# A fourth seven-product block in the second and third column group of w_in

## The reference, cut to what matters

```python
h = rms_norm(x, attn_norm)
z = h @ w_in
r_q, r_k, r_v, r_g, c_q, c_kv, k_pe, g_u, g_v = jnp.split(z, IN_SPLITS, axis=-1)
```

## Time and profile before

| | us |
|---|---|
| median of 3 runs | 1095.73 (1095.42 to 1097.48) |
| profiled execution | 1095.72 |
| its span, first to last instruction | 1093.4 |
| TensorE busy | 1078.3 |
| VectorE busy | 911.8 |
| ScalarE busy | 652.9 |
| GpSimd busy | 55.7 |

### The profile page before, as it was taken

The page is one execution under the profiler, slowest core; times in us unless marked ns, Lnnn a source line. Parts: engine busy times, 40 slices in busy tenths (PEclk is TensorE's granted clock), DMA queues, the critical chain, the costliest instruction groups (busy, mean ns, idle before and its releaser), DMA issues.

```text
span 1093.4 us, 12415 instructions
## 1 busy us (share of the span) xinstructions
PE 1078.3 (99%) x5094; PEld 896.6 (82%) x5094; DVE 911.8 (83%) x859; ACT 652.9 (60%) x638; POOL 55.7 (5%) x54
## 2 busy tenths in 40 slices
PE   9999999999999999999999999999999999999997
PEld 6888889987888877788888888888888778888886
DVE  6879666754566798999999999999999799999994
ACT  7666547665655566655656656556665655565652
POOL 0078000000000000000000000000000000000000
PEclk9999999999999999999999999999999999999999
DMA  8765544644355577677677677677674755555552
GB/s 327 281 236 195 193 135 131 203 156 139 130 180 170 190 269 225 236 231 236 218 237 223 208 241 221 224 234 221 234 234 159 303 192 197 195 205 205 199 195 112
DMA packets 50295, 227.50 MB, mean 208 GB/s; under 512 B 4288, under 2 KB 10176, under 8 KB 28736
## 3 DMA queue, kind: packets, MB, share of 16 engines
q1 hardware_dynamic: 47936, 213.84, 57.2%
q0 software_dynamic: 1440, 10.49, 4.8%
q10 hardware_dynamic: 864, 2.39, 0.6%
HBM read 222.51 MB, written 4.19 MB: 207 GB/s over the span
## 4 chain that ended last, share of the span: by engine, by line
PE 88%; DVE 6%; ACT 2%; DMA 2%; issue 1%; SPq 0%; DVEq 0%; ACTq 0%
PE ps L1676 67%; PE ps L1529 5%; PE ps L1531 5%; PE ps L1530 5%; PE ps L1568 2%; DMA raw<-in_w_dn 1%; DVE w_lo L1239 1%; DVE t_lo L1268 1%; ACT t_hi L747 1%; PE ps L1616 1%; DVE t_sum L1253 1%; PE ps L1793 1%; PE ps L1795 1%; PE ps L1794 1%; PE ps L1615 0%
## 5 line engine op out<-in xcount | busy, mean ns | idle before, releaser
L1676 PE MATMUL ps<-w_hi,xp_hi 128*128 128x512 f32 x404 | 159.8, 395 | 1.8 <-DVE ps L1371 0.7
L966 DVE TENSOR_TENSOR w_lo<-raw,w_hi 128x2048 fp32r<-128x2048 f32 (+2 forms) x42 | 87.3, 2078 | 86.4 <-ACT w_hi L490 86.4
L1676 PE MATMUL ps<-w_hi,xp_lo 128*128 128x512 f32 x404 | 157.5, 390 | 0.0
L1676 PE MATMUL ps<-w_lo,xp_hi 128*128 128x512 f32 x404 | 157.4, 390 | 0.0
L747 ACT ACTIVATE t_hi<-t_sum 128x2048 fp32r<-128x2048 f32 x44 | 84.4, 1918 | 73.3 <-DVE t_sum L1258 73.3
L830 ACT ACTIVATE w_hi<-raw 128x2048 fp32r<-128x2048 f32 (+1 forms) x44 | 79.1, 1798 | 79.7 <-DMA raw<-in_w_dn 79.7
L1676 PE MATMUL ps<-w_hi,xo_hi 128*128 128x512 f32 x292 | 113.9, 390 | 2.1 <-DVE xo_lo L1431 2.1
L1676 PE MATMUL ps<-w_lo,xo_hi 128*128 128x512 f32 x292 | 113.6, 389 | 0.0
L1676 PE MATMUL ps<-w_hi,xo_lo 128*128 128x512 f32 x292 | 113.6, 389 | 0.0
L1268 DVE TENSOR_TENSOR t_lo<-t_sum,t_hi 128x2048 fp32r<-128x2048 f32 x44 | 100.7, 2289 | 6.6 <-ACT t_hi L747 6.6
L490 ACT ACTIVATE w_hi<-raw 128x2048 fp32r<-128x2048 f32 (+2 forms) x42 | 73.0, 1738 | 50.4 <-DMA raw<-in_w_out 25.6
(11 more groups left out here) (294 smaller groups left out, 2456.9 us busy)
## 6 DMA issues: line engine op xcount, KB each, us to landing
raw<-in_w_gu SPq DMA_DIRECT2D x78, 1024.0 KB, 5.0
raw<-in_w_dn SPq DMA_DIRECT2D x44, 1024.0 KB, 4.9
raw<-in_w_i SPq DMA_DIRECT2D x21, 1024.0 KB, 4.9
raw<-in_w_out SPq DMA_DIRECT2D x16, 1024.0 KB, 5.1
raw<-in_w_in SPq DMA_DIRECT2D x12, 1024.0 KB, 5.1
d_raw<-in_w_gu SPq DMA_DIRECT2D x10, 1024.0 KB, 4.8
d_lo<-in_w_gu POOLq DMA_DIRECT2D x10, 1024.0 KB, 11.7
raw<-in_w_in SPq DMA_DIRECT2D x8, 576.0 KB, 3.8
```

What stands on the lines that cost most here:

```text
L966: nc.vector.tensor_tensor(w_lo[n % 4][:, 0:k, 0:c], raw[n % 4][:, 0:k, 0:c], w_hi[n % 4][:, 0:k, 0:c].bitcast(F32), ALU.subtract).then_inc ...
L1676: mm = nc.tensor.matmul(out, x, wt, start=start and j + m == 0, stop=stop and 3 * j + m == n - 1, skip_group_check=resumed)
```

## The change

The pair that stood last in groups 1 and 2 (pair 4) moves to position 5 and becomes a fourth seven-product block, so that positions 0, 2, 4 and 5 are such blocks. Its activation sums are a fourth `xi`, made in group 0. The mixing moves from steps 4 and 5 to step 5, and the operations of `in_lo(n + 3)` are spread between the parts of the mixing. TensorE now waits for the mixed banks at position 7, the last chunk of the group. VectorE gets one more wait: the sums of position 5 use the buffers of position 2, so they wait until TensorE has used that chunk.

```diff
-IN_ORDER = [list(range(8))] + [[5, 0, 6, 1, 7, 2, 3, 4]] * 2
-IN_SUMS = (5, 6, 7)
+IN_ORDER = [list(range(8))] + [[5, 0, 6, 1, 7, 4, 2, 3]] * 2
+IN_SUMS = (5, 6, 7, 4)
+IN_AT = (0, 2, 4, 5)
...
-    return (g - 1) * NI + p // 2 if g and p < 5 and p % 2 == 0 else None
+    return (g - 1) * NI + IN_AT.index(p) if g and p in IN_AT else None
...
                 if n == FB - AHEAD:
                     x_sums_hi(2)
-                if g and p == 4:
+                    x_sums_hi(3)
+                if g and p == IN_AT[-1]:
                     act.wait_ge(in_mix_done, 2 * (g - 1) + 1)
...
-            def in_lo(n):
+            def in_lo(n, parts="swl"):
...
+                if "s" in parts:
+                    dve.wait_ge(raw_in[slot], 16 * (n // 4 + 1))
+                    if n % FB == IN_AT[-1]:
+                        dve.wait_ge(chunk_used, n - IN_AT[-1] + IN_AT[1] + 1)
...
+            x_sums(3)
             x_sums_lo(2)
+            x_sums_lo(3)
             for n in range(FB - AHEAD, C0):
                 g, p = divmod(n, FB)
-                if g and p == 4:
+                if g and p == IN_AT[-1]:
                     in_mix_sums(g)
+                    if n + AHEAD < C0:
+                        in_lo(n + AHEAD, "s")
                     in_mix_banks(g, 0)
-                if g and p == 5:
+                    if n + AHEAD < C0:
+                        in_lo(n + AHEAD, "w")
+                    else:
+                        low(n + AHEAD, c=width(n + AHEAD))
                     in_mix_banks(g, 1)
-                if n + AHEAD < C0:
+                    if n + AHEAD < C0:
+                        in_lo(n + AHEAD, "l")
+                elif n + AHEAD < C0:
                     in_lo(n + AHEAD)
...
-                    if g and p == 6 and b == 0:
+                    if g and p == IN_AT[-1] + 2 and b == 0:
                         pe_.wait_ge(in_mixed, 2 * (g - 1) + half + 1)
```

More of the change, by code:

```diff
@@ L163, in build @@
         xi = [at(f"xi{i}", 64 * K + 4 * K * i, [8, P]) for i in range(NI)]
-        xi_hi = [at(f"xi_hi{i}", H0 + 51 * K + 512 + 4 * K * i, [4, P], F32R) for i in range(NI)]
-        xi_lo = [at(f"xi_lo{i}", H0 + 53 * K + 512 + 4 * K * i, [4, P], F32R) for i in range(NI)]
+        XI_AT = [H0 + 51 * K + 512 + 4 * K * i for i in range(3)] + [152 * K]
+        xi_hi = [at(f"xi_hi{i}", XI_AT[i], [4, P], F32R) for i in range(NI)]
+        xi_lo = [at(f"xi_lo{i}", XI_AT[i] + 2 * K, [4, P], F32R) for i in range(NI)]
         mix_in = at("mix_in", 144 * K, [4, COLS])
@@ L1052, in in_lo @@
                 b12, b22, b21 = raw[slot][:, 0, :], raw[slot][:, 2, :], raw[slot][:, 3, :]
[L1053 to L1065, removed]
+                if "s" in parts:
+                    dve.wait_ge(raw_in[slot], 16 * (n // 4 + 1))
+                    if n % FB == IN_AT[-1]:
+                        dve.wait_ge(chunk_used, n - IN_AT[-1] + IN_AT[1] + 1)
+                    nc.vector.tensor_tensor(t_in[:, 0:2, :], raw[slot][:, 1:3, :],
+                                            b12.unsqueeze(1).to_broadcast([P, 2, COLS]), ALU.add).then_inc(in_sum_step, 1)
+                    dve.wait_ge(in_sum_step, 3 * s + 1)
+                    nc.vector.tensor_tensor(t2, t1, b22, ALU.add).then_inc(in_sum_step, 1)
+                    dve.wait_ge(in_sum_step, 3 * s + 2)
+                    nc.vector.tensor_tensor(t4, t2, b21, ALU.add).then_inc(in_sum_step, 1)
+                if "w" in parts:
+                    dve.wait_ge(in_sum_step, 3 * s + 3)
+                    dve.wait_ge(hi_ready, n + 1)
+                    nc.vector.tensor_tensor(w_lo[slot][:, 1:4, :], raw[slot][:, 1:4, :], w_hi[slot][:, 1:4, :].bitcast(F32),
+                                            ALU.subtract)
+                if "l" in parts:
+                    dve.wait_ge(in_tops_hi, s + 1)
+                    nc.vector.tensor_tensor(t_in_lo[:], t_in[:], t_in_hi[:].bitcast(F32), ALU.subtract).then_inc(lo_ready, 1)
             def in_mix_sums(g):
@@ L1083, in in_mix_banks @@
                 else:
-                    dve.wait_ge(chunk_used, FB * g + 6)
+                    dve.wait_ge(chunk_used, FB * g + IN_AT[-1] + 2)
                     dve.wait_ge(in_mix_step, 3 * g)
@@ L1692, in in_sums @@
                 x = IN_SUMS.index(pair)
-                start, stop = p == 0, p == 4
+                start, stop = p == IN_AT[0], p == IN_AT[-1]
                 tokens = {"a11": (0, slice(0, P)), "a12": (1, slice(0, P)), "a22": (1, slice(P, 2 * P))}
@@ L1729, in in_plain @@
                         pe_.wait_ge(acc_free, 4 * g)
-                    if g and p == 6 and b == 0:
+                    if g and p == IN_AT[-1] + 2 and b == 0:
                         pe_.wait_ge(in_mixed, 2 * (g - 1) + half + 1)
                     mm = in_side(n, b, half, (0, 1), start=g > 0 and p == 1 and side == 3,
-                                 stop=p == FB - 1 or (g > 0 and p == 5), resumed=g > 0 and p > 5)
-                    if g and p == 5 and side == 1:
+                                 stop=p == FB - 1 or (g > 0 and p == IN_AT[-1] + 1),
+                                 resumed=g > 0 and p > IN_AT[-1] + 1)
+                    if g and p == IN_AT[-1] + 1 and side == 1:
                         mm.then_inc(in_part_done, 1)
```

6 lines of the change are left out of this document (3 added, 3 removed).

## The result

The changed kernel takes 1100.85 us (median of 6 runs, 1100.25 to 1101.64), the kernel before 1096.25 in the same comparison (6 runs, 1094.86 to 1098.12). The ratio is 1.0041, with an interval of 1.0028 to 1.0054: slower by some 4.5 us, where 3.3 were predicted. Of the forecast's range, 1096.8 to 1101.0, this is the upper edge. The profiled execution took 1100.25 us, its span 1097.5, against 1095.72 and 1093.4 before.

The account below looks back on a forecast made before the run. TensorE, busy in 99% of the span, was taken as the bound, so only matmuls and its gaps count. -2.11 + 1.4 + 3.9 + 0.1 = +3.3 us on 1095.72 gave 1099.0 us, range 1096.8 to 1101.0.

Parts of the forecast that it names:

- clock rival: Behind the gap at chunk 15 TensorE falls to half rate: +1.9 us, 1100.9, or 1104 if all chunk 15; chance 0.05.
- signs of being wrong: Chunk 15 starting before 89, chunk 24 displaced by something in group 2, or matmuls behind the gap wider than 0.23.
- The saving: Chunks 13 and 21 drop from 24 to 21 matmuls and position 6's 0.75 us gap goes: -2.11 us.
- Group 0 at nothing: The fourth `xi` made in group 0, about 1.5 us of additions, is covered by slack before chunk 8 and costs nothing.
- The wait at chunk 13: Group 1: TensorE waits for `ti_lo` of chunk 13, 1.25 us and a restart of 0.15: +1.4 us.
- The wait at chunk 15: Group 1: TensorE waits for the mixed banks until 91.4, 3.75 us and a restart of 0.15: +3.9 us.
- a shorter second wait: Rival at chunk 15: loads land earlier, first wait vanishes, second stays under 2.9 us: 1096.5 to 1097.9; chance 0.06.
- Group 2 at 0.1: Group 2: `ti_lo` of chunk 21 is done just when TensorE asks: +0.1 us, with 0 and 0.6 as ends.
- The sum: The w_in stage up to chunk 24: -2.11 + 1.4 + 3.9 + 0.1 = +3.3 us, the work behind it unchanged.
- It is hidden: Rival at group 1's first bank add: done by chunk 15's turn, only the saving is left, 1093.6 us; chance 0.12.

Follow-up runs that it names:

- e6: The changed kernel without GpSimd's reduction of the rotary angles (so another output): 1098.22 us, ratio 1.0018 to the kernel before.
- e7: The changed kernel with the decay table's load moved from ahead of the w_in loads to step 18: 1098.24 us, ratio 1.0026 to the kernel before.
- e3: The changed kernel with ScalarE's squares at step 8 and root at step 9, instead of steps 9 to 11: 1097.13 us, ratio 1.0009 to the kernel before.
- e2: The changed kernel with the first bank add ahead of chunk 16's sums in VectorE's list: 1100.24 us, ratio 1.0033 to the kernel before.
- e1: The changed kernel with 14 dummy matmuls on TensorE ahead of its wait at chunk 15: 1099.65 us, ratio 1.0023 to the kernel before.
- e8: The changed kernel with squares and root early, decay load later, both bank adds ahead of chunk 16's `w_lo`: 1097.14 us, ratio 1.0010 to the kernel before.
- e4: The changed kernel with the fourth block in group 2 alone, group 1 as in the kernel before: 1094.63 us, ratio 0.9984 to the kernel before.
- e11: The kernel of e4 (fourth block in group 2 alone) run again unchanged: 1094.83 us, ratio 0.9985 to the kernel before.
- e10: The fourth block in group 2 alone, with squares and root early and the decay load later: 1094.03 us, ratio 0.9974 to the kernel before.
- e5: The kernel before, unchanged, timed against itself and profiled a second time: 1096.19 us, ratio 1.0003.
- e9: The kernel before (three blocks a group) with squares and root early and the decay load later: 1096.73 us, ratio 0.9997 to the kernel before.

## Why the prediction was right, and by how much it was off

**The number.** The direction, the two waits, their places and their releasers were forecast and came. That 1100.85 us lies within 1096.8 to 1101.0 is partly luck: it is above the forecast's own upper end of 1100.2, and it is the price of the clock rival (1100.9), which had a chance of 0.05. One of the prediction's own signs of being wrong, matmuls behind the gap wider than 0.23, was there. Of the 1.85 us by which 1099.0 was too low, 0.5 is the kernel before, 1096.25 in this comparison instead of 1095.72; the rest is the kernel's.

**The saving** (-2.11): right in this profile. Position 6 has no gap in the changed kernel, and chunks 13 and 21 have 21 matmuls.

**Group 0 at nothing**: right; chunk 12's turn and its load came as before.

**The wait at chunk 13** (predicted 1.4, measured 2.08): the right place and releaser, mis-sized. I took 3.0 us for the sums from the earlier trace rows; they took 3.4 (70.07 to 73.47) and began 0.2 later than I had it, and all behind them moved by as much; TensorE was 0.1 early (75.93). e6 shows that this is GpSimd (2.7 without), e7 that it hangs on the landing of chunk 12. The page "SBUF — State Buffer" of the Trainium skill (section "SBUF: two separate sides") has a VectorE operation with two SBUF inputs and a GpSimd instruction that reads SBUF shut each other out for whole instructions. The traces agree that they interfere: every duration of the sums falls to 1.22, 0.69 and 0.69 once GpSimd is out. The longest stretch of one instruction was 0.40 (1.62 against 1.22), a quarter of GpSimd's 1.61 in the earlier trace rows, and no row shows a whole one.

**The wait at chunk 15** (predicted 3.9 with its restart, measured 3.6 and the restart): right, step by step. `w_hi` of chunk 15 started at 80.63 (80.05 predicted), the mixing at 84.97 (84.5), chunk 16's sums at 87.56 (87.1), the bank add ended at 91.69 (91.35), TensorE started at 91.83 (91.4). Each is late by 0.3 to 0.6, which came with the sums of chunk 13. e3 shows ScalarE's queue to be the largest piece, 2.4 of 3.6; e2 that VectorE's order only moves the wait. The rival *a shorter second wait* was mispriced: with no first wait and a second under 2.9 the sum is below +0.9, so at most 1096.6, and not up to 1097.9.

**Group 2 at 0.1**: right for this kernel (0), for a reason that I hadn't given. The later TensorE leaves group 1, the more lead VectorE has in group 2: with chunk 16 started at 98.80 (here), 98.53 (e2) or 98.13 (e7) there is no wait at chunk 21, at 96.49 (e1) one of 0.3, at 94.81 (e3) one of 0.5, at 93.95 (e8) one of 1.3. As an upper end my 0.6 was too low for a kernel that is less late.

**The clock** (a rival at 0.05, +1.9): this was the step that failed. I called the gap too short to matter, from a trace whose longest wait was 2.1 us, which could say nothing of 3.8. It came, on top of the forecast and not in its place, at +1.5, and with a restart of 0.15 in it that I had counted already it is three quarters of the difference between 3.3 and 5.1 in the stage; the rest is chunk 13 (+0.7) less what chunk 15 waited less (0.15) and group 2's 0.1. The page "TensorE: Matmul & The Clock Gate" of the Trainium skill (section "Why this matters for your kernels") warns of half rate after idle gaps of this size. The traces agree at 3.83, 3.46 and 3.17 us, not at the 3.55 of e6's profiled execution.

**The sum.** +3.3 against +5.1 in the stage, +4.1 in the span and 4.5 in the medians. "It is hidden" fell at once: 5.7 us of waits where less than 2.1 were needed.

**What stays open.** e4 and e11 gain 1.6 to 2.2 us where their stages show 0 and 0.3, and e10 gains more (2.7) than its stage (0.7). A part is the choice of executions: the profiled one of the kernel before, 1095.72 us, was 0.5 to 1.1 below the medians of that kernel, and that of e4, 1095.78, was the slowest of its eleven. Against the stage of e5, 128.33, the three gain 1.0, 1.3 and 1.7. But three matmuls are 0.68 and the gap at chunk 21 takes them back, so the rest isn't the block's saving. In the comparison of e4, the runs of the kernel before have mean clocks of 0.997 (12 runs), 0.998 (9) and 0.999 (6), with mean times of 1097.3, 1096.5 and 1095.7 us; all eleven runs of e4 have 0.998 or 0.999. So the kernel before seems to lose clock in some runs. The mixing of group 1 can hardly be the place: it is the same in e4, and e9, with the moves that leave no gap there in e10, has 0.997 in eight of its ten other executions. No profile of the kernel before caught such a run, so where it happens, and why the kernels with the fourth block in group 2 alone don't have such runs, is not shown. Nor is it settled why the gap of e6 left the clock alone in the execution that was profiled.

## What to carry to other kernels

A matmul saved by more sums on VectorE is worth something only if VectorE has the time. Here a block saves TensorE 0.68 us and costs VectorE 4.7, and at 41.2 us of VectorE's work for 40.8 of TensorE's the trade was over before any order was chosen. One block more in group 2 alone was measured faster (0.9984 and 0.9985), but its three matmuls came back as a wait at chunk 21, and what paid isn't shown. When an instruction is put into a queue, ask what stands behind it there: a 1.8 us `ti_hi` ahead of squares and a root made 2.4 of a gap of 3.6 on another engine. And a predicted gap of some 3 us on TensorE should be priced with a stretch at the low clock behind it; if the gap can't be closed, dummy matmuls in it kept the clock here, worth 1.3 us.

## What the runs showed of the hardware

- The granted clock fell to 0.50 within gaps of 3.83 us (changed kernel), 3.17 (e2) and 3.46 (e7), and not in one of 3.55 (e6's profiled execution, its fastest). It stayed low for seven, seven and fourteen matmul spacings: 1.5, 1.6 and 2.8 us lost. Busy TensorE work without use (e1) kept it at 1.00.
- A 512-column float32 pass starts every 0.227 us at the high level and every 0.43 at the low one.
- The same program differed from one execution to the next by 0.7 us in the landing of one 1 MB load (62.57 and 63.27), and by 1.0 us in the stage behind it.
- GpSimd at work stretched VectorE's sums of chunk 13 and others like them from 1.22 to as much as 1.62 us and from 0.69 to as much as 1.00.
